# The second down pass of a feed-forward block reads six more steps through another buffer, the next norm's rows come eight steps later, and a chain of small parameter instructions six products earlier

## What is computed

```python
def swiglu(x, w_in, w_out):
    gate, up = jnp.split(x @ w_in, 2, axis=-1)
    return (jax.nn.silu(gate) * up) @ w_out          # 1024 x 2816 hidden

def first_block(x, ...):
    ...
    h = h + jnp.square(jax.nn.relu(z @ w_up[l])) @ w_down[l]     # hidden 4096
    ...
def second_block(x, ...):
    h = rms_norm_2(x, ffn1_pre_g[l])
    x = x + 0.5 * rms_norm_2(swiglu(h, ffn1_w_in[l], ffn1_w_out[l]), ffn1_post_g[l])
    h = rms_norm_2(x, mix_pre_g[l])
    ...                                              # attention and s5_mixer
def s5_mixer(u, a_re, a_im, log_dt, b_re, b_im, c_re, c_im, ...):
    dt = jnp.exp(log_dt)[:, None]
    a_bar = jnp.exp(dt * (a_re + 1j * a_im))
    b_bar = ((a_bar - 1.0) / a)[..., None] * b
    ...
```

## Time and profile before

| | us |
|---|---|
| median of 3 runs | 2943.12 (2941.12 to 2943.53) |
| the profiled execution | 2944.2 |
| its span in the profile | 2941.9 |
| TensorE busy in the span | 2863.5 (97%) |
| VectorE, ScalarE, GpSimd busy | 1680.6, 1172.8, 476.8 |

### The profile page before, as it was taken

How to read it: one execution, slowest core, us unless ns; L and a number is a source line. 1 busy time by engine, 2 the same in 40 slices (tenths; PEclk the granted TensorE clock), 3 DMA queues, 4 the chain that set the end, 5 groups by cost and what they waited for, 6 DMA issues and landing times.

```text
span 2941.9 us, 35409 instructions
## 1 busy us (share of the span) xinstructions
PE 2863.5 (97%) x13496; PEld 2351.1 (80%) x13496; DVE 1680.6 (57%) x2487; ACT 1172.8 (40%) x1861; POOL 476.8 (16%) x1023
## 2 busy tenths in 40 slices
PE   8999999999999999999998699999999999999999
PEld 7787888888887878888887487887787888888887
DVE  6754766543435578777742534326656866665454
ACT  6524555432324354333331424126654433332332
POOL 0000000010000000688988100012101000000000
PEclk9999999999999999999999799999999999999999
DMA  3123333374442122233253632212124122224543
GB/s 134 43 93 115 100 115 115 109 263 143 147 145 95 45 93 86 88 124 111 108 203 122 223 122 86 72 62 101 53 86 158 59 78 86 86 86 158 168 141 142
DMA packets 100744, 335.76 MB, mean 114 GB/s; under 512 B 12400, under 2 KB 13168, under 8 KB 98272
## 3 DMA queue, kind: packets, MB, share of 16 engines
q1 hardware_dynamic: 82512, 260.08, 25.7%
q0 software_dynamic: 18064, 73.41, 6.7%
HBM read 257.03 MB, written 75.24 MB: 113 GB/s over the span
## 4 chain that ended last, share of the span: by engine, by line
PE 80%; POOL 13%; DMA 2%; DVE 2%; ACT 1%; issue 1%; SPq 0%; DVEq 0%; POOLq 0%; ACTq 0%
PE ps L127 24%; PE ps L129 24%; PE ps L128 24%; POOL tmp_p L1858 2%; POOL tmp_p L1861 2%; POOL tmp_p L1860 2%; POOL tmp_p L1859 2%; POOL made_osc L1862 2%; PE ps L2312 1%; POOL made_osc L1863 1%; PE ps L2327 1%; PE ps L2286 1%; DMA ssm_mid<-made_out 1%; PE ps L267 1%; POOL made_out L1862 1%
## 5 line engine op out<-in xcount | busy, mean ns | idle before, releaser
L127 PE MATMUL ps<-ring_b 128*128 128x512 f32 x832 | 325.8, 392 | 38.7 <-DVE acc L1310 36.9
L129 PE MATMUL ps<-ring_b 128*128 128x512 f32 x832 | 324.7, 390 | 0.0
L128 PE MATMUL ps<-ring_b 128*128 128x512 f32 x832 | 324.7, 390 | 0.0
L127 PE MATMUL ps<-region_a,up_slots 128*128 128x512 f32 x672 | 264.7, 394 | 8.9 <-DVE up_slots L878 8.9
L871 ACT ACTIVATE up_slots<-weight_sums 128x512 fp32r<-128x512 f32 x216 | 136.1, 632 | 319.4 <-PE ps L129 299.2
L128 PE MATMUL ps<-region_a,up_slots 128*128 128x512 f32 x672 | 262.9, 391 | 0.0
L129 PE MATMUL ps<-region_a,up_slots 128*128 128x512 f32 x672 | 262.7, 391 | 0.0
L127 PEld LDWEIGHTS ps<-ring_b 128*128 128x128 f32 x832 | 156.8, 189 | 72.2 <-issue 37.3
L127 PE MATMUL ps<-region_a,region_b 128*128 128x512 f32 x448 | 180.7, 403 | 3.3 <-DVE region_b L122 2.4
L129 PEld LDWEIGHTS ps<-ring_b 128*128 128x128 f32 x832 | 156.7, 188 | 32.7
L128 PEld LDWEIGHTS ps<-ring_b 128*128 128x128 f32 x832 | 156.8, 188 | 32.4
(11 more groups left out here) (430 smaller groups left out, 6388.3 us busy)
## 6 DMA issues: line engine op xcount, KB each, us to landing
raw<-feed SPq DMA_DIRECT2D x212, 512.0 KB, 3.6
raw<-stream SPq DMA_DIRECT2D x56, 512.0 KB, 3.5
far_raw_b<-feed SPq DMA_DIRECT2D x38, 512.0 KB, 4.4
weight_sums<-hid SPq DMA_DIRECT2D x76, 256.0 KB, 3.8
hid_raw<-hid SPq DMA_DIRECT2D x76, 256.0 KB, 3.8
x_mid<-acc POOLq DMA_DIRECT2D x32, 512.0 KB, 3.2
hid<-late_pieces SPq DMA_DIRECT2D x27, 512.0 KB, 2.6
ssm_row<-ssm_mid POOLq DMA_DIRECT2D x8, 1632.0 KB, 7.6
```

Of the source, the lines that this page charges most:

```text
L127: nc.tensor.matmul(psum, lhs(0), rhs(0), start=first, stop=False)
L128: nc.tensor.matmul(psum, lhs(0), rhs(1), start=False, stop=False)
L129: return nc.tensor.matmul(psum, lhs(1), rhs(0), start=False, stop=last)
```

## The change

Three edits. `hid_place` keeps hidden rows in `weight_sums` for the steps up to n+5 (`HID_NEAR` = 6), and the wait for `hid_free` moves with it from steps n and n+1 to n+6 and n+7; this holds for all three blocks. `behind` puts the near rows' hooks at steps n+8 to n+15 (`ROWS_FROM` = 8) in place of n to n+7, for `mlp` and `ffn1`. The seven parameter hooks of `ffn1`'s up pass go six products up each. Nothing is added or removed.

```diff
+        HID_NEAR, ROWS_FROM = 6, 8
...
-            return (weight_sums[:, 0] if kk < F.n else hid_raw)[:, kk % 2, :]
+            return (weight_sums[:, 0] if kk < F.n + HID_NEAR else hid_raw)[:, kk % 2, :]
...
-                if F.n <= kk < F.n + 2:
+                if F.n + HID_NEAR <= kk < F.n + HID_NEAR + 2:
                     for cond in F.hid_free:
                         sp.wait_ge(*cond)
...
-            return {F.n + k: hook for k, hook in hooks.items()}
+            return {F.n + ROWS_FROM + k: hook for k, hook in hooks.items()}
...
-            quick_up_act(act, ffn1, {18: lambda: ssm_step_size_act(act), 24: lambda: ssm_decay_act(act),
-                                     26: lambda: ssm_angle_act(act)})
+            quick_up_act(act, ffn1, {12: lambda: ssm_step_size_act(act), 18: lambda: ssm_decay_act(act),
+                                     20: lambda: ssm_angle_act(act)})
...
-            quick_up_dve(dve, ffn1, {20: lambda: ssm_angle_dve(dve), 30: lambda: ssm_growth_dve(dve),
-                                     34: lambda: ssm_inverse_dve(dve), 38: lambda: ssm_factors_dve(dve)})
+            quick_up_dve(dve, ffn1, {14: lambda: ssm_angle_dve(dve), 24: lambda: ssm_growth_dve(dve),
+                                     28: lambda: ssm_inverse_dve(dve), 32: lambda: ssm_factors_dve(dve)})
```

## The result

| | before | after |
|---|---|---|
| median, us | 2942.36 (2941.12 to 2943.53) | 2903.47 (2903.22 to 2904.05) |
| span of the profiled execution, us | 2941.9 | 2901.8 |
| TensorE busy, us | 2863.5 (97%) | 2860.2 (99%) |
| GpSimd busy, us | 476.8 | 487.0 |

The ratio of after to before is 0.9868, 95% interval 0.9851 to 0.9885: 38.9 us faster by the medians. The forecast was 2904.0. The median of before is 2942.36 with a fourth execution; it was 2943.12 with the three that the forecast had. Lines behind the first edit are one number higher in the changed kernel, so L1250 of before is L1251 here.

The account below looks back on a forecast made before the run. TensorE, busy for 97% of the span, was taken as the bound, with one stop at ffn1's boundary behind GpSimd's late store. Stop and low clock, 39.6 us, less 0.1 gave 39.5 off: 2904.0 us, range 2901 to 2912.

Parts of the forecast that it names:

- The stop and its worth: At ffn1's second down pass TensorE starts 37.07 us late, plus 2.52 us of low clock; 39.5 us won after 0.1 lost.
- GpSimd's shift: In ffn1's up pass, parameter hooks six products earlier start GpSimd and all its blocks 16.3 us earlier, bounds 14 and 17.5.
- GpSimd beside VectorE: Without the stop, GpSimd's last block runs beside a working VectorE: 51.9 to 54.0 us for 41.7, 10.2 to 12.3 later.
- T: Landing of GpSimd's last table store, which releases SyncE's transfers: 1626.5 before, 1620.4 forecast, bounds 1619.2 to 1624.8.
- The limit: Latest T without a TensorE stop at ffn1's step n+6, complete at T + 13.5 and wanted at 1642.6: 1629.1.
- Edits 2 and 3 at no cost: Near rows done by about 1697, transposes at 1716, cost nothing; parameter hooks in the busy up pass nothing, at most 1.6 us.
- The rivals: GpSimd still late at step n+6 (0.10), hooks not bringing GpSimd forward (0.03), slower (0.03), no gain (0.02).
- The hooks don't bring GpSimd forward: GpSimd waits for something else, T stays at 1636.7, TensorE stops 7.6 us at n+6: 2911.6 to 2914, chance 0.03.
- The slower rival: Near rows are late for the transposes in the second pass's last section and TensorE stops; example 2953 us, chance 0.03.

Follow-up runs that it names:

- the kernel with the old parameters: The changed kernel with ffn1's parameter hooks back at their old products, 18 to 38: 2911.36 us.
- The thinned VectorE: The changed kernel, but in ffn1's down steps up to n+5 VectorE subtracts 64 of 1024 columns for the weights' low part: 2903.16 us, one execution.
- five steps: The changed kernel with five steps' hidden rows in the norm's buffer in place of six: 2903.83 us.
- four steps: The changed kernel with four steps' hidden rows in the norm's buffer in place of six: 2905.09 us.
- three products: The changed kernel with the parameter hooks three products up in place of six: 2902.95 us.
- two steps: The changed kernel with two steps' hidden rows in the norm's buffer in place of six: 2915.75 us.
- the earlier start: The changed kernel with only the parameter hooks moved up, no steps in the norm's buffer and near rows at n to n+7: 2927.42 us.

## Why the prediction was right

**The stop and its worth.** The forecast was 37.07 us of stop and 2.52 us of low clock, less 0.1 at the boundary. At the same point late in the second pass, a wait of 0.89 us for VectorE, TensorE stands at 1750.62 in the profile of before and at 1710.53 in that of after: 40.1 us earlier. Of this, 0.8 us were there before the boundary (the first pass's last matmul starts at 1608.99, and at 1609.76 in before), and belong to the two executions. 39.3 us are the change's. Forecast 39.5. The boundary costs 0.2 us, twice what I took and within its bounds. The medians give 38.9.

**GpSimd's shift.** GpSimd's wait for the parameters fell from 108.0 to 91.7 us, forecast some 92, so GpSimd starts 16.3 us earlier, as forecast. The store of the seventh block moved by 1581.52 - 1564.68 = 16.8 us, the 0.8 us between the two executions included.

**GpSimd beside VectorE.** The last block took 50.2 us; I had taken 51.9 to 54.0. That the block would be longer than in the profile of before was the step on which the margin most depended, and the kernel with the old parameters shows it alone: 51.3 us. The thinned VectorE shows the cause.

**T, by misses that partly cancel.** The store was issued at 1614.9, where 1617.1 was forecast (16.3 earlier, 10.2 longer); it took 7.4 us to land, where I took the 3.28 of the earlier trace rows. T was 1622.3, forecast 1620.4, within the bounds of 1619.2 to 1624.8. That it fell within them is in part luck: my bounds held the landing fixed, and with the block at its longest the store would have landed past them, at 1628.9, just short of the limit of 1629.1. The trace of before could have told me, since its other seven stores of this kind landed 3.3 to 5.0 us after their issue.

In before, SyncE had issued nothing for 42 us when the last store went out; here, steps n+4 and n+5 had been issued 2.4 and 0.5 us ahead, and the old rows followed. The other traces fit that. With the near rows from n+3, where two steps had again just gone out, the landing was 7.7 us; with five steps, where only step n+4 had, 4.2; with the old parameters, with four steps and with three products, where SyncE's last step was 16, 15 and 8 us old, 3.3 us again. In every run but that of the changed kernel one store of the sixth or seventh block went out less than 1 us behind the last transfer of a step: these eleven landed after 4.9 to 6.5 us, the other one of each pair after 3.6 to 4.9. That points to the company of those transfers. It was not isolated, and it is not the whole: with two steps the last store took 4.5 us, though SyncE had issued nothing for 22. The rule of the Trainium skill that I had weighed (SBUF — State Buffer, section "SBUF: two separate sides") puts a longer store beside a two-port VectorE copy down to descriptors that GpSimd can't write. The issue took 0.59 us as before, and VectorE ran nothing between 1614.4 and 1619.1, so the trace again doesn't show that.

**The limit.** I had 1629.1 for T. Step n+6 was complete 12.6 us after T, forecast 13.5. So step n+6 was 7.1 us ahead of TensorE, forecast 8.7 (1629.1 - 1620.4). The kernels with five and four steps bracket that margin.

**Edits 2 and 3 at no cost.** The last `xn` row was done at 1695.3, forecast 1697; the transposes come at 1716.8, forecast 1716. In the early up pass VectorE rose from 17.81 to 18.80 us busy of 20 and TensorE stayed at 20.00.

```profile
1120.00:1140.00 20.00, 20.00 (x90) 16.55 (x89) 18.80 (x38) 11.95 (x19) 0.00 (x0) 1.00 0.23 79
```

**The rivals.** None came. "The hooks don't bring GpSimd forward" was priced at 2911.6 to 2914; the kernel with the old parameters, which has that effect, takes 2911.36. The slower rival's mechanism showed in the kernel with the rows at n+14.

## What to carry to other kernels

When a helper engine's long job ends a stop, its duration in that profile is flattering: it ran its last part beside idle engines. Take the job's length from a stretch in which the others work, here 50 to 54 us for 42, before counting the slack that a move needs. The same holds for the transfer that ends the job, here 7.4 us for 3.3. And price the two halves of such a change together. Alone, the earlier start was worth 14.3 us, and the later deadline without it came to 7.9 us short of the whole; together they win 38.9, and five steps with six products, or six steps with three, win the same.

## What I had not expected of the hardware

- GpSimd's block grew from 42.5 and 44.4 us to 54.7 and 50.2 by VectorE's 128x1024 subtractions of two SBUF operands at one in 5.44 us, about a quarter of VectorE's time. The Trainium skill, SBUF — State Buffer, section "Who interferes with whom", says that a VectorE instruction with two SBUF inputs contends with a GpSimd instruction that reads SBUF, and calls what they share an exclusive lock. The traces agree: 21.8 us less of VectorE over the two blocks, 18.2 us of GpSimd back, and a GpSimd instruction of 0.61 us that takes 1.48 beside a subtraction. Whether it is the second SBUF input that matters, no run here separates.
- A store of GpSimd that lands in 3.3 us alone took 7.4 and 7.7 us right behind two steps' transfers.
- Behind a stop of TensorE the low clock cost 2.5 us after 36.9 us of idling, 1.8 after 24.0, 2.5 after 9.0, 1.7 after 5.8, 2.3 after another of 5.8 and 1.7 after 1.8: it does not grow with the stop, and a stop of 1.8 us can cost as much again.
